# Attention on one Trainium2 core: VectorE takes the score maxima first, and norms and rotates later queries between and behind them

## The reference, cut to what matters

```python
qa = rms_norm(qa.reshape(B, T, ATT_HEADS, HEAD_DIM), q_g)   # per head, head_dim 64
q_att = axial_rope(qa, rows)                                # latent tokens only
k_all = jnp.concatenate([k_c, axial_rope(ka, rows)], axis=1)
s = jnp.einsum('bqkgd,bskd->bkgqs', qblk, k).astype(jnp.float32) * scale
p = jax.nn.softmax(s, axis=-1).astype(v.dtype)
return jnp.einsum('bkgqs,bskd->bqkgd', p, v)
```

## Time and profile before

| what | us |
|---|---|
| median of three runs | 3431.66 |
| the profiled execution, its own time | 3425.92 |
| its span, first to last instruction | 3423.8 |
| mean granted TensorE clock over the span | 0.96 of full speed |
| the two attention stretches, about | 457 to 745, and 2168 to 2456 |

### The profile page before, as it was taken

The page is one execution under the profiler, slowest core; times in us unless marked ns, Lnnn a source line. Parts: engine busy times, 40 slices in busy tenths (PEclk is TensorE's granted clock), DMA queues, the critical chain, the costliest instruction groups (busy, mean ns, idle before and its releaser), DMA issues.

```text
span 3423.8 us, 44625 instructions
## 1 busy us (share of the span) xinstructions
PE 3131.3 (91%) x17048; PEld 2525.3 (74%) x17048; DVE 1689.5 (49%) x3156; ACT 947.7 (28%) x1834; POOL 488.3 (14%) x608
## 2 busy tenths in 40 slices
PE   4999969989899999999968989699898999999997
PEld 3788834448788888889857878344487999999995
DVE  4446666645533333333384366666455333333337
ACT  2222334442411121112222222344424122222212
POOL 3012223321100000000041022233211000000003
PEclk7999979999999999999979999699999999999999
DMA  5440120002222222221321101100021111111103
GB/s 206 151 128 27 60 74 0 0 25 93 77 88 79 81 79 72 85 80 39 111 98 35 51 28 67 65 0 0 25 96 62 38 50 50 37 38 50 50 25 147
DMA packets 100999, 220.07 MB, mean 64 GB/s; under 512 B 13264, under 2 KB 16144, under 8 KB 100304
## 3 DMA queue, kind: packets, MB, share of 16 engines
q1 hardware_dynamic: 78240, 151.76, 14.0%
q0 software_dynamic: 19952, 62.40, 5.0%
q10 hardware_dynamic: 2624, 3.41, 0.3%
HBM read 191.00 MB, written 26.51 MB: 64 GB/s over the span
## 4 chain that ended last, share of the span: by engine, by line
PE 75%; DVE 9%; issue 7%; DMA 3%; POOL 3%; ACT 2%; DVEq 1%; POOLq 1%; ACTq 0%; SPq 0%
PE ps L1584 21%; PE ps L1587 20%; PE ps L1588 20%; PE ps L1781 3%; PE ps L1760 2%; DVE nm L1359 2%; PE ps L1566 2%; PE ps L1771 1%; DVE hf L1022 1%; PE ps L1772 1%; POOL dg L630 1%; DVE w_lo L460 1%; PE ps L1696 1%; PE ps L1691 1%; DMA w_raw<-in_w_slots 1%
## 5 line engine op out<-in xcount | busy, mean ns | idle before, releaser
L1584 PE MATMUL ps<-hi,w_hi 128*128 128x384 f32 x1584 | 539.9, 341 | 36.3 <-DVEq L398 18.4
L1588 PE MATMUL ps<-hi,w_lo 128*128 128x384 f32 x1584 | 533.1, 337 | 0.0
L1587 PE MATMUL ps<-lo,w_hi 128*128 128x384 f32 x1584 | 532.7, 336 | 0.0
L1584 PE MATMUL ps<-w_hi,f_hi 128*128 128x512 f32 x1152 | 457.5, 397 | 18.4 <-DVE acc L1488 18.4
L1587 PE MATMUL ps<-w_lo,f_hi 128*128 128x512 f32 x1152 | 451.0, 392 | 0.0
L1588 PE MATMUL ps<-w_hi,f_lo 128*128 128x512 f32 x1152 | 450.4, 391 | 0.0
L455 ACT CAST w_hi<-w_raw 128x512 fp32r<-128x512 f32 x368 | 213.4, 619 | 766.4 <-PE ps L1584 715.9
L1488 DVE TENSOR_TENSOR acc<-acc,ps 128x512 f32<-128x512 f32 x288 | 196.1, 685 | 419.2 <-PE ps L1588 419.0
L1584 PE MATMUL ps<-w_hi,hi 128*128 128x512 f32 (+1 forms) x1008 | 390.1, 387 | 9.1 <-ACT stg L739 5.8
L1588 PE MATMUL ps<-w_hi,lo 128*128 128x512 f32 (+1 forms) x1008 | 381.8, 379 | 0.0
L1587 PE MATMUL ps<-w_lo,hi 128*128 128x512 f32 (+1 forms) x1008 | 381.7, 379 | 0.0
(11 more groups left out here) (271 smaller groups left out, 4210.7 us busy)
## 6 DMA issues: line engine op xcount, KB each, us to landing
w_raw<-in_w_slots SPq DMA_DIRECT2D x368, 256.0 KB, 3.0
w_raw<-in_m_slots SPq DMA_DIRECT2D x160, 256.0 KB, 2.9
x_dram<-xr POOLq DMA_DIRECT2D x18, 512.0 KB, 3.1
x1t<-x_dram POOLq DMA_DIRECT2D x6, 1536.0 KB, 14.3
out<-acc POOLq DMA_DIRECT2D x18, 512.0 KB, 3.0
modw<-in_w_mod SPq DMA_DIRECT2D x4, 2048.0 KB, 9.8
acc<-in_x_in SPq DMA_DIRECT2D x3, 1536.0 KB, 17.1
zq_dram<-stg POOLq DMA_DIRECT2D x18, 256.0 KB, 2.4
```

The costliest lines, as they stand in the source:

```text
L1584: mm = pe.matmul(out, a_hi, b_hi, start=first, stop=False)
L1587: pe.matmul(out, a_hi, b_lo, start=False, stop=False)
L1588: return pe.matmul(out, a_lo, b_hi, start=False, stop=last)
```

## The change

On VectorE, and on no other engine, the work of `queries` is cut into three parts instead of two: 0 is the norm, 1 the three multiplications of the rotation, 2 the addition and the copy (`doubled`), which begin with the drain that stood between. The table `PREP` places them: the norm goes from in front of the first maximum to behind it; nothing is placed behind the second; the multiplications stay behind the third; the addition and copy, which raise `qd_done`, go from in front of the fourth maximum to behind it. For the prompt tile the single copy L1345 goes from in front of the fourth maximum to behind it as well. A drain is added between all this and `outputs`, in every step with `nn`. The calls ahead of the walk (`queries(0, 0)`, `queries(0, 1)`) run all three parts in sequence, as before.

```diff
--- before.py
+++ after.py
@@ -61,6 +61,7 @@
 NG = 2 * NT
 N_E = 2 * (NS * NT + 1)
 SCORES_AT = {0: 0, 1: 1, 2: 2, 4: 3}
+PREP = ((0,), (), (1,), (2,))
 
 
 
@@ -1306,6 +1307,9 @@
                         d4 = qd[:, a:a + nh, 1, r * h_:(r + 1) * h_].rearrange("p a (b c) -> p a b c", b=2)
                         s4 = rp[:, t, 1, r * h_:(r + 1) * h_].rearrange("p (b c) -> p b c", b=2)
                         dve.tensor_tensor(d4, q4[:, :, ::-1, :], spread(s4, nh), ALU.mult)
+
+                def doubled(nh, a):
+
                     dve.drain()
                     dve.tensor_tensor(qd[:, a:a + nh, 0], qd[:, a:a + nh, 0], qd[:, a:a + nh, 1], ALU.add)
                     dve.drain()
@@ -1336,16 +1340,20 @@
                     ins = dve.tensor_copy(kd[:, 0:NS, v, 1], kd[:, 0:NS, v, 0])
                 ins.then_inc(S["kd_done"], 1)
                 outputs_m(NS)
-                def queries(t, g, part=2):
+                def queries(t, g, parts=range(3)):
+
 
                     o = g * HG
-                    if part != 1:
+                    sample = not (isinstance(t, int) and t == NS)
+                    if 0 in parts:
                         normed(t, HG, ZQ + o * HD, o, 0, HD ** -0.5)
-                    if part and isinstance(t, int) and t == NS:
+                    if 1 in parts and sample:
+                        rotated(t, HG, o)
+                    if 2 in parts and sample:
+                        doubled(HG, o).then_inc(S["qd_done"], 1)
+                    elif 2 in parts:
                         dve.tensor_copy(qd[:, o:o + HG], qn[:, 0:HG * HD].rearrange("p (a b) -> p a b", b=HD).unsqueeze(2)
                                         .broadcast_to([P, HG, 2, HD])).then_inc(S["qd_done"], 1)
-                    elif part:
-                        rotated(t, HG, o).then_inc(S["qd_done"], 1)
 
                 def queries_lo(G, g):
                     dve.wait_ge(S["q_hi_done"], G + 1)
@@ -1383,12 +1391,12 @@
                     if nn:
                         queries_lo(G + 1, 1 - g)
                     dve.drain()
-                    if prep is not None:
-                        queries(prep, g, 0)
                     for h in range(HG if nn else 0):
                         maximum(G + 1, 1 - g, h, nn)
-                        if prep is not None and h == 2:
-                            queries(prep, g, 1)
+                        if prep is not None:
+                            queries(prep, g, PREP[h])
+                    if nn:
+                        dve.drain()
                     if pk:
                         outputs(t if g else t - 1, 1 - g, G - 1, pk)
```

## The result

The changed kernel took 3442.55 us (median of six runs, 3434.14 to 3445.48), the kernel before beside it 3430.16 us (six runs). The ratio is 1.0032 with a 95% interval of 1.0021 to 1.0042. Ten more executions in another session gave 3441.27 against 3431.52 us, ratio 1.0026, interval 1.0013 to 1.0039. The change costs 12.4 us in the first session and 9.8 in the second. The forecast was 3435.5 us and no difference that can be measured; the time lies inside its range (3424 to 3447), but both ratios lie above the bound of 0.2%, on the side to which I gave 22%.

The account below looks back on a forecast made before the run. TensorE, busy 91% of the span, was taken as the bound. Per layer 6 x (0.06 + 0.15) + 0.2 + 0.8 - 0.6 = 1.7 us, twice 3.4, about +4 on the median 3431.66: 3435.5 us, range 3424 to 3447.

Parts of the forecast that it names:

- the bound of 0.2%: Whole kernel: smallest difference a measurement can tell from no change, 6.9 us, or 0.22 us per step over 32 steps.
- the side to which I gave 22%: Whole kernel: the changed kernel measurably slower than before, chance 0.22, against 0.65 for the same and 0.13 for faster.
- The first maximum first: Second head's scores: with the first maximum ahead of the norm they start at 508.82 instead of 509.38, 0.56 us won.
- The norm behind the first maximum: Third head's scores: GpSimd's first sum holds the norm, so they start 0.66 us late, 0.74 in every second step.
- The shift: Shift L1777: addition and copy behind the fourth maximum win 0.60 us; step still 0.06 longer, 0.15 in every second one.
- The steps written out: Steps outside the loop: t = 0, 0 to +0.2 us each; t = 7, +0.8 and -0.6; t = 8, 0.
- The tail: Outputs after the fourth maximum: 1.1 us of work put ahead, end at 520.6 or 520.9, hidden before query transposes at 521.01.
- the cover of 0.1: Query transposes L1749: time left between the end of the outputs and 521.01 if the diagonal holds the addition, 0.1 us.
- TensorE waiting at L1749: Query transposes: the forecast had no wait for the outputs there; a wait would show it wrong.
- The rival of the tail: Query transposes L1749 wait for outputs if added work is over 0.4 us longer; 0.35 per loop step, 3444 us; chance 0.12.

Follow-up runs that it names:

- small_sum2: The change with GpSimd's first sum of a step over 64 of its 512 columns: 3411.73 us, ratio 0.9935 to the kernel before.
- unrolled: The change with the hardware loop over t = 1 to 6 written out: 3428.25 us, ratio 0.9993 to the kernel before.
- no_drain: The change without its added drain: 3434.56 us, ratio 1.0009 to the kernel before.
- all_idle: The change with all three parts of the queries in front of queries_lo and no added drain: 3399.63 us, ratio 0.9906 to the kernel before.

## Why the prediction was right in its parts and wrong in its sum

- **The first maximum first.** Predicted 0.56 won at the second scores; measured 0.58 (2.82 to 2.24), and 0.51 as the mean of twelve steps. Right.
- **The norm behind the first maximum.** Predicted that the first sum holds L1293, that it ends 0.28 behind the sum, L1296 a little held, third scores 0.66 or 0.74 late. Measured: 1.53 us, 0.29 behind, L1297 0.46, and 0.64 late in the step shown, 0.73 as the mean. Right, and small_sum2 shows the cause. The Trainium skill, page "SBUF — State Buffer", section "Who interferes with whom", says that a VectorE instruction with two SBUF inputs contends with a GpSimd one that reads SBUF; the traces agree, with 1.53 against 0.43 us. The same section of the Trainium skill has the one that comes second blocked for the whole instruction of the first. Here the held L1294 ends 0.29 behind the sum, less than its own 0.42. If it takes 0.42 from its turn on, that turn comes some 0.13 before the sum's logged end (an estimate).
- **The shift.** Predicted 0.06 or 0.15 late, 0.10 as the mean, with the diagonal held; measured 0.04 early in the step shown and 0.05 late as the mean. I took VectorE to be first at the fourth diagonal, after the row at 721.33. It was GpSimd, in all 28 attention steps in which the two meet: the diagonal kept its 0.40 and the addition L1314 took 0.67. The starts are 0.01 apart in both cases, and the winners are not the same.
- **The steps written out.** t = 7: predicted +0.8 and -0.6, measured +0.88 (15.44 to 16.32) and -0.65 (15.49 to 14.84) between shifts. Right.
- **The tail. This is the step that failed.** The prediction had the outputs end at 520.6 or 520.9 against transposes at 521.0, "hidden, by 0.1 to 0.4". From the end of the fourth maximum to the end of the outputs it was 3.11 us (530.95 to 534.06) where I had 1.1 + 1.73 = 2.83, or 3.1 with the addition held. So the later end was the true one, because the diagonal holds the addition. TensorE then starts the transposes no less than 0.15 behind the outputs. I had no time for that, and with it the cover of 0.1 is gone. What was not in the sum at all is that TensorE's sequencer has to be ahead when the loop turns: 0.33 in every second step. The runs unrolled (no turn, 0.38 from a held transpose to the next scores) and no_drain (released earlier, 0.46 to 0.53 at the turn) show both terms apart.

Per loop step: predicted 0.06 and 0.15, mean 0.10; measured 0.36. From the first scores to the shift it is 0.05 of that, where 0.10 was predicted. Behind the shift it is 0.31, where nothing was: 0.14 is the later start of L1757, 0.16 the longer way from there to the next scores (0.32 or more at a turn, 0.03 elsewhere), and 0.01 lies behind. TensorE waiting at L1749 was one of the prediction's own signs of being wrong. The rival of the tail was the right one in its place. It had 0.12, with 0.35 per loop step on top and 3444 us; the run gave 0.26 on top and 3442.55. Its condition was not met, though: the tail had to be over 0.4 longer than 1.1 and was 0.28 longer, so neither the forecast nor the rival had the turn or the 0.15. What spoke for it in the working, cover of only 0.1 with two instructions and a drain put in front of it, should have made it the forecast.

## What to carry to other kernels

A VectorE instruction that took 0.42 us with GpSimd idle took 1.5 beside GpSimd's sum: put such instructions where GpSimd is idle, and look at its timeline before moving them. Here the same instructions in another place took the ratio from 1.0026 to 0.9906 and 0.9891 (two sessions), and the step from 16.73 to 15.17 us. Where a queue waits on a semaphore close to the turn of a hardware loop, count the turn as work behind that wait; a cover of 0.1 us is none. And measure the halves of a change apart: one of these two was worth -0.4%, the other +0.7%.

The version that beats both is all_idle: ratio to the kernel before 0.9906 (interval 0.9891 to 0.9922), 3399.63 us, in one session and 0.9891 (0.9876 to 0.9906), 3395.03 us, in another.

## What the runs showed of the hardware that was not expected

- From the transposes to the next scores TensorE took 0.67 to 0.75 us where the loop turns, once its sequencer had been held at the semaphore just ahead, against 0.35 when nothing held it; 0.46 to 0.53 when the sequencer was released 0.1 to 0.2 us before TensorE was ready (no_drain); and 0.38 with the wait but without a turn (unrolled, at 607.55). With the sequencer 1.2 us ahead nothing of the turn is seen.
- Two requests 0.01 us apart, GpSimd's logged first each time, went once to VectorE (sum 1.56, L1296 0.43) and 28 times to GpSimd (diagonal 0.40, L1314 0.67). So which of two such requests is first can't be read from the logged starts; what decides it stays open.
- Single executions of one and the same kernel differ by 16 us with the mean granted clock (3424.1 at 0.961, 3440.6 at 0.954), more than the whole effect. Medians of several runs, and step lengths from traces, were needed to see it.
